# Delta rule's triangular inverses: products up to blocks of 64 as two 64x64x64 products in opposite quarters of the PE array

## What is computed

```python
a = jnp.einsum('bhnid,bhnjd->bhnij', k_beta, k) * decay
a = jnp.where(strict, a, 0.0) + jnp.eye(c, dtype=a.dtype)
u = lax.linalg.triangular_solve(a, v_beta, left_side=True, lower=True, unit_diagonal=True)
w = lax.linalg.triangular_solve(a, k_beta * jnp.exp(gc)[..., None],
                                left_side=True, lower=True, unit_diagonal=True)
```

## Time and profile before

| | |
|---|---|
| median of 3 runs | 2001.51 us (1999.73 to 2002.68) |
| profiled execution | 2005.06 us, of which 2003.2 us are the span from its first to its last instruction |
| mean granted clock of TensorE | 0.983 |
| busy in the span | PE 96%, PEld 80%, DVE 73%, ACT 62%, POOL 3% |
| HBM | 260 GB/s over the span; the DMA queues are idle during the levels |
| the six levels | 390.8 to 454.1 us of the span |

### The profile page before, as it was taken

The page is one execution under the profiler, slowest core; times in us unless marked ns, Lnnn a source line. Parts: engine busy times, 40 slices in busy tenths (PEclk is TensorE's granted clock), DMA queues, the critical chain, the costliest instruction groups (busy, mean ns, idle before and its releaser), DMA issues.

```text
span 2003.2 us, 25946 instructions
## 1 busy us (share of the span) xinstructions
PE 1932.5 (96%) x9350; PEld 1605.8 (80%) x9350; DVE 1472.3 (73%) x1286; ACT 1236.1 (62%) x1085; POOL 68.4 (3%) x108
## 2 busy tenths in 40 slices
PE   7999999898999999999999999999996899999999
PEld 6888877796788888888888888888874788788887
DVE  5654656676689888988989888898885546676554
ACT  5544556322477777777777787777764457645443
POOL 0000001000100000000000000000022100000000
PEclk9999999998999999999999999999998999999999
DMA  8974533001399999999999999999984332245452
GB/s 310 365 282 147 210 144 130 1 1 74 129 415 361 383 390 361 411 364 393 363 384 392 369 402 359 391 381 371 392 314 163 142 136 87 103 147 205 176 188 83
DMA packets 76923, 521.82 MB, mean 260 GB/s; under 512 B 8240, under 2 KB 8496, under 8 KB 17584
## 3 DMA queue, kind: packets, MB, share of 16 engines
q1 hardware_dynamic: 72512, 504.02, 65.3%
q0 software_dynamic: 4192, 16.25, 2.1%
q10 hardware_dynamic: 144, 0.52, 0.1%
HBM read 501.37 MB, written 19.40 MB: 260 GB/s over the span
## 4 chain that ended last, share of the span: by engine, by line
PE 75%; DVE 5%; ACT 3%; issue 1%; POOL 1%; DMA 0%; DVEq 0%; SPq 0%; ACTq 0%; POOLq 0%
PE bank L809 15%; PE bank L810 15%; PE bank L814 15%; PE bank L506 6%; PE bank L523 6%; PE bank L507 6%; PE bank L579 4%; PE bank L831 1%; DVE w_lo L1842 1%; POOL small L1741 1%; ACT w_hi L1274 1%; DVE kT L1922 0%; PE bank L556 0%; DVE xT L1873 0%; PE bank L657 0%
## 5 line engine op out<-in xcount | busy, mean ns | idle before, releaser
L2175 DVE TENSOR_TENSOR w_lo<-raw,w_hi 128x2048 fp32r<-128x2048 f32 x336 | 762.6, 2289 | 111.3 <-ACT w_hi L1437 108.4
L1437 ACT ACTIVATE w_hi<-raw 128x2048 fp32r<-128x2048 f32 x336 | 643.4, 1919 | 143.8 <-PE bank L814 143.7
L1842 DVE TENSOR_TENSOR w_lo<-raw,w_hi 128x2048 fp32r<-128x2048 f32 (+2 forms) x136 | 298.0, 2198 | 165.9 <-ACT w_hi L1274 164.6
L1274 ACT ACTIVATE w_hi<-raw 128x2048 fp32r<-128x2048 f32 (+2 forms) x136 | 249.3, 1840 | 172.4 <-PE bank L523 159.6
L809 PE MATMUL bank<-w_hi,xT 128*128 128x512 f32 x896 | 353.8, 395 | 0.0
L810 PE MATMUL bank<-w_hi,xT 128*128 128x512 f32 x896 | 349.6, 390 | 0.0
L506 PE MATMUL bank<-w_hi,xT 128*128 128x512 f32 (+1 forms) x784 | 314.3, 402 | 20.6 <-DVE xT L1873 9.7
L507 PE MATMUL bank<-w_hi,xT 128*128 128x512 f32 (+1 forms) x784 | 308.8, 395 | 0.0
L814 PE MATMUL bank<-w_lo,xT 128*128 128x512 f32 x896 | 240.0, 390 | 0.0
L814 PEld LDWEIGHTS bank<-w_lo,xT 128*128 128x128 f32 x896 | 168.3, 188 | 35.3
L810 PEld LDWEIGHTS bank<-w_hi,xT 128*128 128x128 f32 x896 | 168.5, 188 | 33.7
(11 more groups left out here) (413 smaller groups left out, 1935.6 us busy)
## 6 DMA issues: line engine op xcount, KB each, us to landing
raw<-in_experts_dram SPq DMA_DIRECT2D x336, 1024.0 KB, 7.0
raw<-in_tiles_dram SPq DMA_DIRECT2D x125, 1024.0 KB, 4.8
rows_in<-zeros POOLq DMA_DIRECT2D x1, 6144.0 KB, 32.7
rows_out<-zeros POOLq DMA_DIRECT2D x1, 5632.0 KB, 55.3
raw<-in_tiles_dram SPq DMA_DIRECT2D x9, 512.0 KB, 3.5
item_rows<-rows_in SPq DMA_DIRECT2D x7, 512.0 KB, 7.3
rows_out<-y_s SPq DMA_DIRECT2D x7, 512.0 KB, 3.6
row<-in_rows_dram SPq DMA_DIRECT2D x1, 1040.0 KB, 14.6
```

What stands on the lines that cost most here:

```text
L1274: nc.scalar.activation(w_hi[:, i % SPL, 0:kc * w], raw[:, i % DENSE, 0:kc * w], ACT.Copy)\
L1437: nc.scalar.activation(w_hi[:, w_slot(j), :], raw[:, raw_slot(j), :], ACT.Copy).then_inc(m_hi, 1)
L1842: nc.vector.tensor_tensor(w_lo[:, i % SPL, 0:kc * w], raw[:, i % DENSE, 0:kc * w], w_hi[:, i % SPL, 0:kc * w], ALU.subtract).then_inc(spli ...
L2175: nc.vector.tensor_tensor(w_lo[:, s, :], raw[:, raw_slot(j), :], w_hi[:, s, :], ALU.subtract).then_inc(m_lo, 1)
```

## The change

For levels 1 to 5 all blocks of T, TT, dec and X lie in the two diagonal quarters of 64x64, since the blocks joined are at most 64 wide. The change computes these quarters alone. Each 128x128x128 product becomes two of 64x64x64, one on partitions 0 to 63 and columns 0 to 63, one on 64 to 127 both ways. The copy of X on ACT and the two subtractions on DVE become two instructions each of 64 partitions by 4 x 64 columns. The mask (`level`) stays whole. Level 6 stays as it was, with the off-diagonal quarters of T and TT zero as they were first written. In the changed kernel L506, L579, L703, L1342 and L1984 are one or more lines further down (L507, L580, L704, L1349, L1997).

```diff
@@ -47,6 +47,7 @@
 
 
 LEVELS = (1, 2, 4, 8, 16, 32, 64)
+BLOCKS = (slice(0, P // 2), slice(P // 2, P))
 CONST_AT = {}
 _at = 0
 for _name, _n in (("ident", P), ("ones", P), ("upto", P), ("before", P), ("from_", P), ("future", P),
@@ -702,22 +703,28 @@
                         for k in range(4):
                             last = nc.tensor.transpose(b[:, k * P:k * P + P], buf["TT", tt, hg][:, k, :], ident)
                         last.then_inc(tp_done, 1)
+                def level_products(name, owner, l, left, right):
+
+                    if l == len(LEVELS) - 1:
+                        small_products(name, owner, lambda b: [
+                            (o, left[:, k, :], right[:, k, :]) for k, o in enumerate(four(b))])
+                    else:
+                        small_products(name, owner, lambda b: [
+                            (o[r, r], left[r, k, r], right[r, k, r]) for k, o in enumerate(four(b)) for r in BLOCKS])
+
                 for l in range(1, len(LEVELS)):
                     for g, (tt, hg) in enumerate(GROUPS):
 
                         pe.wait_ge(inv_level, (l - 1) * len(GROUPS) + g + 1)
                         result(("T", tt, hg) if l == 1 else ("inv_T", tt, hg, l - 1))
-                        small_products(("X", tt, hg, l), "A", lambda b: [
-                            (o, buf["dec", tt, hg][:, k, :], buf["T", tt, hg][:, k, :]) for k, o in enumerate(four(b))])
+                        level_products(("X", tt, hg, l), "A", l, buf["dec", tt, hg], buf["T", tt, hg])
                     for tt, hg in GROUPS:
                         result(("X", tt, hg, l))
                         if l > 1:
                             result(("inv_TT", tt, hg, l - 1))
                         if l < len(LEVELS) - 1:
-                            small_products(("inv_T", tt, hg, l), "D", lambda b: [
-                                (o, buf["TT", tt, hg][:, k, :], buf["X", tt, hg][:, k, :]) for k, o in enumerate(four(b))])
-                        small_products(("inv_TT", tt, hg, l), "D", lambda b: [
-                            (o, buf["X", tt, hg][:, k, :], buf["TT", tt, hg][:, k, :]) for k, o in enumerate(four(b))])
+                            level_products(("inv_T", tt, hg, l), "D", l, buf["TT", tt, hg], buf["X", tt, hg])
+                        level_products(("inv_TT", tt, hg, l), "D", l, buf["X", tt, hg], buf["TT", tt, hg])
                 for tt in range(NT):
                     now = slice(tt * P, tt * P + P)
                     for hg in range(2):
@@ -1402,7 +1409,13 @@
                 for l in range(1, len(LEVELS)):
                     for tt in range(NT):
                         for hg in range(2):
-                            keep(("X", tt, hg, l), buf["X", tt, hg][:, :, :])
+                            if l == len(LEVELS) - 1:
+                                keep(("X", tt, hg, l), buf["X", tt, hg][:, :, :])
+                                continue
+                            b = batch(("X", tt, hg, l))[:, :].rearrange("p (a b) -> p a b", a=4)
+                            for r in BLOCKS:
+                                tell(nc.scalar.activation(buf["X", tt, hg][r, :, r], b[r, :, r], ACT.Copy),
+                                     tp_free["A"] if r.start else a_own)
                 for tt in range(NT):
                     for hg in range(2):
                         keep(("vnew", tt, hg), buf["X", tt, hg][:, :, :])
@@ -2013,11 +2026,16 @@
                     for tt in range(NT):
                         for hg in range(2):
                             T, TT = buf["T", tt, hg][:, :, :], buf["TT", tt, hg][:, :, :]
-                            if l < len(LEVELS) - 1:
-                                tell(nc.vector.tensor_tensor(T, T, bank4(("inv_T", tt, hg, l)), ALU.subtract), tp_free["D"])
-                            tell(nc.vector.tensor_tensor(TT, TT, bank4(("inv_TT", tt, hg, l)), ALU.subtract), tp_free["D"])
-                            if l < len(LEVELS) - 1:
-                                level(l + 1, tt, hg)
+                            if l == len(LEVELS) - 1:
+                                tell(nc.vector.tensor_tensor(TT, TT, bank4(("inv_TT", tt, hg, l)), ALU.subtract),
+                                     tp_free["D"])
+                                continue
+                            for name, x in (("inv_T", T), ("inv_TT", TT)):
+                                b = bank4((name, tt, hg, l))
+                                for r in BLOCKS:
+                                    tell(nc.vector.tensor_tensor(x[r, :, r], x[r, :, r], b[r, :, r], ALU.subtract),
+                                         tp_free["D"] if r.start else d_own)
+                            level(l + 1, tt, hg)
                 for tt in range(NT):
 
                     for hg in range(2):
```

## The result

| | before | after |
|---|---|---|
| first comparison, median | 2001.29 us (5 runs) | 2009.95 us (5 runs, 2005.54 to 2011.60) |
| second comparison, median | 2001.32 us (17 runs) | 2008.09 us (12 runs, 2002.15 to 2011.25) |
| profiled execution | 2005.06 us, span 2003.2 | 2010.21 us, span 2008.4 |
| its mean granted clock | 0.983 | 0.982 |

The change makes the kernel slower. The first comparison gives a ratio of 1.0041 (95% interval 1.0027 to 1.0054), which is +8.7 us (5.4 to 10.8); the second 1.0031 (1.0019 to 1.0043), +6.8 us (3.8 to 8.6). The forecast was 2007.3, slower, with 2001.5 to 2013.0 as its range.

The account below looks back on a forecast made before the run. DVE's and PE's loops were taken as level at 11.02 us per level, DVE's deciding after the change. Start and five loops summed to 12.5p - 4.2 = +5.8 us at a batch length p of 0.8: 2001.5 + 5.8 = 2007.3 us, range 2001.5 to 2013.0.

Parts of the forecast that it names:

- Two loops level, DVE decides: Per level, DVE's loop (8.81 + 2.21 = 11.02 us) equals PE's 12 batches of 0.915; the change's effect on DVE's loop decides.
- DVE 10.24 us per level: DVE's work in a level with subtractions in halves of 425 ns: 10.24 us in place of 8.67.
- p = 0.8: Length in us of a new PE batch of 16 short pairs in levels 1 to 5, 0.05 per pair; bounds 0.46 and 1.06.
- I expect the clock to hold: PE's granted clock in the levels: with PE busy for 79% at a 0.8 us batch, it would not fall.
- rival 2: Levels 1 to 6: 0.46 us batches leave PE half idle, clock halves, gap 2.27 us; +8.9 us, chance 0.15.
- busy brings the clock back: Argument against a full effect of the fallen clock: a slow PE is a busy one, which restores the clock; no size given.
- 12.5p - 4.2: Total difference in us over start and five loops, p being a new PE batch's length: +5.8 at 0.8, +1.6 at 0.46.
- the switch at level 6: On PE, going from products over 64 rows back to whole ones at level 6 costs 0.2 us once.
- its two terms at level 6: Fallen-clock costs at level 6: 0.9 us for its own gap, and 2.5 taken of up to 4 x 0.9 at its end.
- The switch of tiling: On PE, changing between products over 128 and 64 rows costs 0.2 us, once at level 1 and once at level 6.
- Rivals 3 and 4: PE, levels 1 to 5: short pair costs as much as long, +35 us, 0.08; each quarter change costs 0.2 us, +101, 0.04.
- Rival 5: DVE's halves cheaper than the rows say: 0.30 us instead of 0.425 needed to gain 4 us; chance 0.01.

Follow-up runs that it names:

- dve_halves_only: Kernel before with only DVE's subtractions split in halves, PE products and ACT copies whole: 2009.78 us, ratio 1.0033.
- pe_halves_only: The change with DVE's subtractions and ACT's copies whole again, only PE's products in quarters: 1996.76 us, ratio 0.9970 against the kernel before.
- one_quarter: The change without the lower quarter's products in levels 1 to 5, 8 pairs per batch: 2007.95 us in one run.
- compact: The change with both quarters on the same 64 columns in levels 2 to 4, level 6 computing one quarter: 1983.38 us, ratio 0.9905 against the kernel before.

## Why the prediction was right in sign and wrong in a step

**Two loops level, DVE decides: right.** `dve_halves_only` alone brings a loss as large as the change's, `pe_halves_only` a gain.

**DVE 10.24 us per level: right, a little high.** It was 10.11. A half took 418 ns, not 425. ACT's copies were 378 ns (expected 383) and nobody waited for them in the loops; the one place where they held PE is level 1's start, for 0.2 us.

**p = 0.8: wrong.** The step that failed is the choice between the ends: "the nearest row is the 0.066, since 16 pairs have to be issued where 8 were, and overlap of the quarters can only take a part off". A pair takes 29 ns on average at the full clock and the overlap is complete (`one_quarter`): p = 0.465. Two tiny transposes were no bound for two products in opposite quarters. PE's timeline of the change, around the start of a batch at 396.31, in two windows that take in the first two and the first six of its matmuls:

```profile
396.31 0.23 PE L580 MATMUL bank<-TT,X 64*64 64x64 f32 x2
...
396.31 0.34 PE L580 MATMUL bank<-TT,X 64*64 64x64 f32 x6
```

One such matmul lasts 0.22 us, so the two quarters of a head start within 0.01 us of each other, and the next couple follows some 0.058 later: 0.465 / 8. The Trainium skill (TensorE: Matmul & The Clock Gate, "Part 3: Packing small matmuls — row/col tiling") says that such products run at the same time and start some 4 ns apart. For the two of a couple the trace agrees, as far as 0.01 us can tell. What sets p is the distance of the couples, 58 ns, which holds a weight load and a matmul in each quarter.

**"I expect the clock to hold": wrong**, and it hung on the same step. With p = 0.465 PE is busy for half of a level, as rival 2 says, and the clock fell at all four turns in one execution and at two in another. Its gap was priced at 2.27 and was 2.14. But level 6 kept the full clock (4.75 us in the chain, as before), so the 2.5 that rival 2 put at its end did not come, nor level 6's own 0.9 (gap 2.21). Where the clock was low there, in `one_quarter`, that gap was 3.04, 0.83 longer. The same run answers rival 2's "busy brings the clock back": PE was busy for 55.88 of the 61.00 us from 394.50 to 455.50 and the clock stayed at 0.50. What brought it back in the change, the runs don't show.

**The sum.** It can be made again with what was measured, in the forecast's own terms. At p = 0.465, 12.5p - 4.2 = +1.6. The gaps at the lower clock add 4 x (2.14 - 1.32) = 3.3. DVE's loops are 5 x 0.13 = 0.65 shorter, and the switch at level 6 (0.2) cost nothing: the load at 448.96 follows 0.12 us behind the T that releases it, as elsewhere (0.11). Together +4.1. The trace has +4.2: the loops 61.31 - 55.12 = +6.2, and the start -2.0 (2.86 us from where the loads could have begun, 391.05, in place of 4.84; 391.05 is the 390.76 of before with the 0.29 us by which all work ahead came later). The forecast's +5.8 came close by luck, because two errors cancel in the loops: a gap of 1.9 from slow batches at a fast clock, where it was 2.14 from fast batches at a slow one. With DVE's smaller loops the five loops come to +6.2 both in the forecast (4 x 12.17 + 12.65 - 55.12) and in the trace. The 1.6 by which the forecast lies over the trace's +4.2 is the start, -2.0 where p = 0.8 gives -0.4. **The truth in the levels was rival 2 (0.15) without its two terms at level 6**: p = 0.465 and the lower clock at the turns. The two things that the forecast rested on, p = 0.8 and a clock that holds, were both wrong.

**The switch of tiling: right at the start.** The first small product waits 0.17 us "on issue" at 391.24. The rows that I priced it by, L945 to L946, go the other way, from 64 rows to 128, so the agreement is in part luck. Rivals 3 and 4 fell with p. Rival 5 fell with the 418 ns.

**What the sum doesn't hold.** The two comparisons say +8.7 and +6.8; the levels account for +4.2, or +2.5 in an execution whose clock holds at two of the four turns. The second interval holds the 4.2, the first doesn't. Between the two profiled executions, 5.2 us apart, there is no further cost in the 100 us behind the levels (101.61 and 101.57); the rest is 0.3 ahead of the levels and 0.7 behind 566 us. But executions of one kernel differ by more than the effect. The two profiled ones of the changed kernel have spans of 2008.4 and 2000.3 us. 1.7 of those 8.1 lie between the levels' first T and level 6's TT (61.31 and 59.65), 1.6 in the first wait behind, and 5.6 in the 100 us after that (101.57 and 95.95), at a granted clock of 0.93 and 0.98; 1.0 lies behind that, and ahead of the levels the shorter one is 1.8 behind the other.

The runs of the second comparison point the same way by their mean clock. Of the kernel before, 13 of 17 had 0.985 to 0.989 and took 1997.32 to 2002.41 us, and four had 0.981 to 0.983 and took 2005.57 to 2007.48. Of the change, 10 of 12 had 0.977 to 0.982 and took 2006.80 to 2011.25, and two had 0.984 and 0.985 and took 2003.23 and 2002.15. So the 6.8 us between the medians may be the levels' 2.5 to 4.2 and, for the rest, a lower clock outside them in more executions of the change. That is not shown: of the kernel before only an execution with the mean clock 0.983 was profiled.

## What to carry to other kernels

When two loops are level, price a change on the loop that it lengthens, and only then on the one that it shortens: taking work off PE gained nothing here that DVE's extra instructions and the lower clock did not take back. Splitting a result by partitions costs the engine that reads it a full instruction for each part, since time goes with columns; place the parts under one another in the same columns, and the same split halves the reading too (in `compact` the levels in that form bring 12.4 of its 18 us). And an engine that is made faster and left waiting may get the lower clock at the worst moment, in the few instructions that the next stage waits for: 0.81 us at a turn, all of it won back by dummy products that kept PE busy.

## What I had not expected of the hardware

- Two products of 64x64x64 in opposite quarters cost what one costs: a batch of 16 pairs 0.85 us, one of 8 pairs in one quarter 0.855, both at 1.2 GHz; at 2.4 GHz the 16 take 0.465.
- The overlap partly survives an order that puts four products of one quarter in a row (0.57 to 0.76 us a batch).
- The clock at the same step of two levels can be 1.00 and 0.50 within one execution, worth 0.82 us of a level of 12.25.
- With products in one quarter alone the clock stayed at 0.50 for 61 us, though PE was busy for 55.88 of them (`one_quarter`).
